# Second attention's results leave PSUM as a high and a low part, and the first weights of the next two products are loaded and split one stage earlier

## The reference, cut to what matters

```python
outs = []
for s0 in range(0, S, Q_BLOCK):              # causal attention, 8 heads
    s = einsum("bqhd,bkhd->bhqk", q[:, s0:e], k[:, :e]) * scale
    p = softmax(where(mask, s, -inf))
    outs.append(einsum("bhqk,bkhd->bqhd", p, v[:, :e]))
o = concatenate(outs).reshape(B, S, 8 * 128)
branch_b = o @ w_mla_o                        # 1024 x 1024
merged = sigmoid(g_a) * branch_a + sigmoid(g_b) * branch_b
h = h + merged @ w_out                        # 1024 x 1024
h = h + hier_moe_2(rmsnorm(h, norm2_g), ...)  # router and experts
```

## Time and profile before

| | us |
|---|---|
| median of three runs (lowest, highest) | 3392.04 (3391.34, 3392.91) |
| the profiled execution's own time | 3380.64 |
| span of its instructions | 3379.1 |
| second attention (`mla_attention`) | from 2294.9 to 2558.8 |
| `merged_product` | from 2559.3 to 2659.7 |
| `residual_norm` of the second block | from 2660.3 on |

### The profile page before, as it was taken

The page is one execution under the profiler, slowest core; times in us unless marked ns, Lnnn a source line. Parts: engine busy times, 40 slices in busy tenths (PEclk is TensorE's granted clock), DMA queues, the critical chain, the costliest instruction groups (busy, mean ns, idle before and its releaser), DMA issues. The chain is left out here.

```text
span 3379.1 us, 41934 instructions
## 1 busy us (share of the span) xinstructions
PE 2882.8 (85%) x16732; PEld 1827.3 (54%) x16732; DVE 1291.4 (38%) x2499; ACT 868.7 (26%) x1446; POOL 309.8 (9%) x490
## 2 busy tenths in 40 slices
PE   5999989777969999994899989787898896878783
PEld 2888667656833333334777877344567772333231
DVE  5321078765731111116365212456554453111113
ACT  5211055573100000005355202233334210100001
POOL 0210000001001110102000000130001101111112
PEclk8999999988979999997999999998999997989897
DMA  7222198042379999976311312200003529999997
GB/s 275 55 81 81 44 412 327 12 164 97 118 287 383 405 405 392 405 322 248 93 46 42 100 60 87 75 11 1 1 1 131 182 97 386 420 420 421 418 414 302
DMA packets 201762, 694.42 MB, mean 206 GB/s; under 512 B 28883, under 2 KB 76934, under 8 KB 151670
## 3 DMA queue, kind: packets, MB, share of 16 engines
q1 hardware_dynamic: 161542, 587.46, 44.8%
q0 software_dynamic: 27520, 75.53, 5.8%
q10 hardware_dynamic: 12528, 29.01, 2.2%
HBM read 579.02 MB, written 138.07 MB: 212 GB/s over the span
## 5 line engine op out<-in xcount | busy, mean ns | idle before, releaser
L2421 PE MATMUL exp_ps_g<-exp_raw,exp_xT 128*32 128x512 f32 x3072 | 337.0, 596 | 9.5 <-ACT exp_xT L2467 9.5
L2725 PE MATMUL exp_ps_g<-exp_gu,exp_xT 128*64 128x512 f32 x992 | 255.1, 673 | 88.3 <-DMA exp_gu<-in_exp_w 83.1
L2421 PEld LDWEIGHTS exp_ps_g<-exp_raw,exp_xT 128*32 128x32 f32 x3072 | 116.8, 110 | 213.7 <-issue 199.3
L2725 PEld LDWEIGHTS exp_ps_g<-exp_gu,exp_xT 128*64 128x64 f32 x992 | 84.3, 154 | 239.3 <-issue 206.7
L724 PE MATMUL inproj_ps<-inproj_w_low,h1T_high 128*128 128x512 f32 (+1 forms) x448 | 178.8, 399 | 9.7 <-DVE inproj_w_low L434 9.7
L726 PE MATMUL inproj_ps<-inproj_w_high,h1T_high 128*128 128x512 f32 (+1 forms) x448 | 175.5, 392 | 0.0
L725 PE MATMUL inproj_ps<-inproj_w_high,h1T_low 128*128 128x512 f32 (+1 forms) x448 | 174.7, 390 | 0.0
L2445 PE MATMUL exp_ps_y<-exp_raw,exp_hT 128*32 128x512 f32 x1536 | 169.8, 592 | 0.8 <-DVE exp_hT L2511 0.8
L2504 DVE TENSOR_TENSOR exp_h<-exp_sg,exp_ps_g 128x512 f32<-128x512 f32 x24 | 26.0, 1085 | 341.9 <-ACT exp_sg L2473 341.9
L2893 DVE TENSOR_TENSOR exp_h<-exp_sg,exp_ps_g 128x256 f32<-128x256 f32 x32 | 19.6, 611 | 337.2 <-ACT exp_sg L2818 337.2
L2757 PE MATMUL exp_ps_y<-exp_dn,exp_hT 128*64 128x512 f32 x512 | 115.8, 592 | 1.5 <-DVE exp_hT L2900 1.5
(11 more groups left out here) (543 smaller groups left out, 5812.1 us busy)
## 6 DMA issues: line engine op xcount, KB each, us to landing
exp_gu<-in_exp_w SPq DMA_DIRECT2D x62, 2048.0 KB, 29.2
exp_raw<-in_expert_w_gate SPq DMA_DIRECT2D x64, 1024.0 KB, 16.6
exp_raw<-in_expert_w_up SPq DMA_DIRECT2D x64, 1024.0 KB, 16.7
exp_raw<-in_expert_w_down SPq DMA_DIRECT2D x64, 1024.0 KB, 15.0
exp_dn<-in_exp_w SPq DMA_DIRECT2D x32, 2048.0 KB, 27.1
scratch_y<-da_zero SPq DMA_DIRECT2D x1, 32768.0 KB, 149.5
scratch_y<-da_zero SPq DMA_DIRECT2D x1, 24576.0 KB, 67.8
open_slab<-in_w_ada SPq DMA_DIRECT2D x16, 1024.0 KB, 14.6
```

Source lines behind the costliest of these rows:

```text
L2421: last = nc.tensor.matmul(ps_g[lane, z], xT[:, n % 2, k, lane], raw[:, of_lane[l], j * F:(j + 1) * F], start=(k == 0), stop=(k == KD - 1))
L2725: last = nc.tensor.matmul(ps_g[side(e)], xT[:, m.par, k, side(e)], gu[:, m.buf, :, e, k, :], start=(k == 0), stop=(k == KD - 1))
```

## The change

The attention's result is no longer copied out of PSUM as it is: ACT casts four heads into the high part of `mla_oT` (`keep_high`), and DVE then makes the low part from PSUM (`keep_low`). Both stand at the end of their iteration, behind the exponentials and the maxima, and `keep_low` waits for `keep_high`. The splitting at the head of `merged_product` is gone. The first slab of `w_mla_o` is loaded and split at the head of `mla_attention` (`FirstSlab`): SP issues it first, ACT splits before its first exponential and DVE before its first maximum. In `merged_product`, SP issues the first three row blocks of `w_out` behind the `ga` of slab 1, and two more at its end; ACT and DVE split two of them behind slabs 2 and 3 (`SplitWeights`). `residual_norm` goes on from there. It takes its weights as four pairs of two blocks each; in the first block's use nothing is loaded or split earlier. The pair `mla_oT` is now placed over `qnT`'s memory.

```diff
-def residual_norm(core, name, hT, w, x, gate, out, gain, shift, rows_out, router, choice, rt, w_pair=None, late=()):
+class SplitWeights:
+    RB, EACH = 3, 2
...
+    def load(self, sp, k):
+        if k >= self.RB:
+            sp.wait_ge(self.split, k - self.RB + 1)
+        sp.dma_start(self.raw[:, k % self.RB], self.rows[:, k]).then_inc(self.loaded[k % self.RB], 16)
+
+    def split_high(self, act, k):
+        act.wait_ge(self.loaded[k % self.RB], 16 * (k // self.RB + 1))
+        self.core.nc.scalar.copy(self.high[k // self.EACH][:, k % self.EACH], self.raw[:, k % self.RB]).then_inc(self.high_done, 1)
+
+    def split_low(self, dve, k):
+        dve.wait_ge(self.high_done, k + 1)
+        high, low = (t[k // self.EACH][:, k % self.EACH] for t in (self.high, self.low))
+        low_part(self.core.nc, low, self.raw[:, k % self.RB], high).then_inc(self.split, 1)
+
+def residual_norm(core, name, hT, weights, x, gate, out, gain, shift, rows_out, router, choice, rt, late=()):
...
-                for k in range(KD):
...
+                for k in range(weights.asked, KD):
+                    weights.load(sp, k)
...
+                for k in range(weights.ready, KD):
+                    weights.split_high(act, k)
...
+                for k in range(weights.ready, KD):
+                    weights.split_low(dve, k)
...
+def mla_attention(core, name, qnT, knT, qrT, krT, v, rq, o_pair, next_slab):
...
+            @block.sync
+            def _(sp):
+                next_slab.load(sp)
...
-                for n in range(0, len(units) + LAG, 2):
-                    if n >= LAG:
+                def keep_high(n):
+                    qt, h = units[n]
+                    if h % 4 == 3:
+                        act.wait_ge(o_done, n + 1)
+                        nc.scalar.copy(high[:, h - 3:h + 1, qt * P:(qt + 1) * P], ps_o[:, h - 3:h + 1]).then_inc(o_high, 1)
+
+                next_slab.split_high(act)
+                for n in range(0, len(units) + LAG + 2, 2):
+                    if LAG <= n < len(units) + LAG:
                         for m in range(2):
                             copy_turned(act, nc.scalar.copy, 0, n - LAG + m)
                     if n < len(units):
                         for m in range(2):
                             exponential(n + m)
+                    if n > LAG:
+                        keep_high(n - LAG - 1)
...
-                def read_results(n):
+                next_slab.split_low(dve)
+                def keep_low(n):
                     qt, h = units[n]
                     if h % 4 == 3:
-                        dve.wait_ge(o_done, n + 1)
-                        V.tensor_copy(qnT[:, h - 3:h + 1, qt * P:(qt + 1) * P], ps_o[:, h - 3:h + 1]).then_inc(o_read, 1)
+                        toks = slice(qt * P, (qt + 1) * P)
+                        dve.wait_ge(o_high, 2 * qt + h // 4 + 1)
+                        low_part(nc, low[:, h - 3:h + 1, toks], ps_o[:, h - 3:h + 1], high[:, h - 3:h + 1, toks]).then_inc(o_read, 1)
...
-                    if n > LAG:
-                        read_results(n - LAG - 1)
...
+                    if n > LAG:
+                        keep_low(n - LAG - 1)
...
+class FirstSlab:
...
+        self.raw = ctx.enter_context(core.nc.sbuf_tensor(f"{name}_raw", [P, KD, P], F32, side="right"))
+        self.high, self.low = pair(core, ctx, f"{name}_w_first", [P, KD, P], "right")
+
+    def load(self, sp):
+        sp.dma_start(self.raw[:], self.w[:, :, 0:P]).then_inc(self.loaded, 16)
+
+    def split_high(self, act):
+        act.wait_ge(self.loaded, 16)
+        self.core.nc.scalar.copy(self.high[:], self.raw[:]).then_inc(self.high_done, 1)
+
+    def split_low(self, dve):
+        dve.wait_ge(self.high_done, 1)
+        low_part(self.core.nc, self.low[:], self.raw[:], self.high[:]).then_inc(self.split, 1)
...
+def merged_product(core, name, oT, first_slab, aT, gT, mT, next_weights):
...
                     if c >= 1:
                         sp.wait_ge(w_split, c)
-                    sp.dma_start(raw[:], wv[:, :, c * P:(c + 1) * P]).then_inc(w_in, 16)
+                        sp.dma_start(raw[:], wv[:, :, c * P:(c + 1) * P]).then_inc(w_in, 16)
...
+                    if c == 1:
+                        for k in range(next_weights.RB):
+                            next_weights.load(sp, k)
+                for k in range(next_weights.RB, next_weights.RB + 2):
+                    next_weights.load(sp, k)
...
                 pe.wait_ge(w_split, 1)
                 for k in range(KD):
-                    pe.wait_ge(o_split, k + 1)
...
-                for k in range(KD):
-                    nc.scalar.copy(o_h[:, k], o[:, k]).then_inc(o_high, 1)
-                    if k == 0:
-                        split(0)
                 split(1)
                 gates(0)
...
                     if c + 2 < KD:
                         split(c + 2)
+                    if c in (2, 3):
+                        next_weights.split_high(act, c - 2)
...
-                for k in range(KD):
-                    dve.wait_ge(o_high, k + 1)
-                    low_part(nc, o_l[:, k], o[:, k], o_h[:, k]).then_inc(o_split, 1)
-                    if k == 0:
-                        split(0)
...
+                    if c in (2, 3):
+                        next_weights.split_low(dve, c - 2)
                 dve.wait_ge(merged, KD)
+        next_weights.asked, next_weights.ready = next_weights.RB + 2, 2
```

More of the change, by code:

```diff
@@ L1775, in number, with __init__, place_raw, place @@
         return nc.gpsimd.memset(self.gp[:], -3.0e38)
-def residual_norm(core, name, hT, w, x, gate, out, gain, shift, rows_out, router, choice, rt, w_pair=None, late=()):
+class SplitWeights:
+    RB, EACH = 3, 2
+    def __init__(self, core, name, w):
+        self.core, self.name = core, name
+        self.rows = w.rearrange("(k p) n -> p k n", p=P)
+        self.loaded = [core.sem(f"{name}_w_in{b}") for b in range(self.RB)]
+        self.high_done, self.split = core.sem(f"{name}_w_high"), core.sem(f"{name}_w_split")
+        self.raw, self.high, self.low = None, [], []
+        self.asked = self.ready = 0
+    def place_raw(self, ctx, side="left"):
+        self.raw = ctx.enter_context(self.core.nc.sbuf_tensor(f"{self.name}_raw", [P, self.RB, D], F32, side=side))
+    def place(self, ctx, upto, side="left"):
+        for k in range(len(self.high) * self.EACH, upto, self.EACH):
+            high, low = pair(self.core, ctx, f"{self.name}_w{k}", [P, self.EACH, D], side)
+            self.high.append(high)
+            self.low.append(low)
+    def load(self, sp, k):
[10 more added lines that the diff above has]
+def residual_norm(core, name, hT, weights, x, gate, out, gain, shift, rows_out, router, choice, rt, late=()):
     nc = core.nc
@@ L1782, in residual_norm @@
     G, GE = wg.shape[1], wg.shape[1] + we.shape[1]
-    wv = w.rearrange("(k p) n -> p k n", p=P)
-    RB, XB, HB = 3, 3, 2
-    w_in = [core.sem(f"{name}_w_in{b}") for b in range(RB)]
+    XB, HB = 3, 2
     x_in = [core.sem(f"{name}_x_in{b}") for b in range(XB)]
@@ L1789, in residual_norm @@
     late_in = core.sem(f"{name}_late_in")
-    w_high, w_split = core.sem(f"{name}_w_high"), core.sem(f"{name}_w_split")
+    w_split = weights.split
     done = core.sem(f"{name}_done")
@@ L1804, in residual_norm @@
         sb = lambda n, s, d=F32: ctx.enter_context(nc.sbuf_tensor(f"{name}_{n}", s, d))
-        raw = sb("raw", [P, RB, D])
-        w_h, w_l = pair(core, ctx, f"{name}_w", [P, KD, D]) if w_pair is None else w_pair
+        if weights.raw is None:
+            weights.place_raw(ctx)
+        weights.place(ctx, KD)
+        raw, w_h, w_l = weights.raw, Joined(weights.high, weights.EACH), Joined(weights.low, weights.EACH)
         xt, yt, ht = sb("x", [P, XB, D]), sb("y", [P, XB, D]), sb("h", [P, HB, D])
@@ L4011, in mla_attention @@
     copied = [sem("copied_act"), sem("copied_dve")]
-    o_done, o_read = sem("o_done"), sem("o_read")
+    o_done, o_high, o_read = sem("o_done"), sem("o_high"), sem("o_read")
+    high, low = o_pair
     barred = sem("barred")
@@ L4181, in merged_product @@
         sb = lambda n, s, d=F32: ctx.enter_context(nc.sbuf_tensor(f"{name}_{n}", s, d))
-        raw = sb("raw", [P, KD, P])
-        w_h, w_l = pair(core, ctx, f"{name}_w", [P, BUF, KD, P])
+        second = pair(core, ctx, f"{name}_w_second", [P, KD, P])
+        w_h, w_l = (first_slab.high, second[0]), (first_slab.low, second[1])
         a, ga, gb = sb("a", [P, BUF, T]), sb("ga", [P, T]), sb("gb", [P, BUF, T])
@@ L4233, in split @@
                         act.wait_ge(done, c - BUF + 1)
-                    nc.scalar.copy(w_h[:, c % BUF], raw[:]).then_inc(w_high, 1)
+                    nc.scalar.copy(w_h[c % BUF][:], raw[:]).then_inc(w_high, 1)
                 def gates(c):
@@ L4269, in split @@
                     dve.wait_ge(w_high, c + 1)
-                    low_part(nc, w_l[:, c % BUF], raw[:], w_h[:, c % BUF]).then_inc(w_split, 1)
```

(20 more changed lines are left out.)

28 lines of the change are left out of this document (10 added, 18 removed).

## The result

The changed kernel took 3397.78 us (median of 14 runs, 3393.67 to 3400.7) against 3391.94 for the one before (14 runs, 3383.7 to 3395.16). The ratio is 1.0024, 95% interval 1.0017 to 1.0031: slower by 5.8 us by the medians and by 8.1 by the ratio, where 3.1 were forecast. That lies in the range. But the forecast called it no difference, with its line at 0.2% or 6.8 us; the measured loss lies about on that line, and an interval that begins at 1.0017 makes it a small loss and not nothing. The profiled execution took 3400.70 us, span 3399.0, 20 us more than the one of before; 10.7 us of these had gathered before the attention stage began (2305.66 in place of 2294.92), ahead of the stages that this text is about. The nine traces that share the change's code there reach that stage between 2297.5 and 2311.6.

The account below looks back on a forecast made before the run. PE was taken to set the pace in the product, with about 36 us of waits in attention; 4.7 + 6.7 - 2.0 - 6.3 = +3.1 on 3392.04 gave 3395.1 us, range 3387 to 3403.

Parts of the forecast that it names:

- Step 1: Head of attention: the first maximum waits behind the first slab's transfer, cast and low part, +4.7 us.
- Step 2: Inside attention: 14 ACT casts at 0.48 us each, between second exponential and copy, delay PE in full, +6.7 us.
- The casts hidden: Rival in attention: PE has other work there, the casts cost 0, sum -3.6 us, 3388.4; chance 0.12.
- DVE's low part: Rival in attention: PE waits for DVE's copy after each `keep_low`, up to +9.5 us, 3404.6; chance 0.10.
- Step 3: First gap and merged product: PE starts 5.4 us earlier, then waits 4 for slab 2's weights; -2.0 us in all.
- the loss of clock behind the stall: Merged product: the clock may fall in the stall at slab 2, losing 2 us once more; half a chance.
- the side chain: Merged product: slower than PE by 0.5 us a slab and 2.4 ahead, bounding the part's gain at -2.9 us.
- The rival of shared transfers: Merged product: transfers share engines, so slab 1's `ga` lands late; part becomes +3.3 us, sum +8.4, 3400.4; chance 0.12.
- Step 4: Second gap, before the residual stage: two row blocks ready, PE starts 5.9 us earlier, clock -0.4; -6.3 us.
- Step 5: `residual_norm` of the first block and the pair over `qnT`: same instructions, only addresses move; no cost.

Follow-up runs that it names:

- e2_slab_late: Changed kernel with the first weight slab still loaded at attention's head but split by ACT and DVE behind its exponentials and maxima: 3389.62 us, 1.0002 to the kernel before.
- e1_cast_early: Changed kernel with ACT's cast of four heads moved ahead of the two exponentials of its iteration: 3388.97 us, ratio 0.9998 to the kernel before.
- the repeated run: The changed kernel measured once more with no edit: 3397.49 us, ratio 1.0027 to the kernel before.
- e3_order: Changed kernel with the three `w_out` row blocks issued behind the third slab's weights instead of ahead of them: 3397.1 us, ratio 1.0024 to the kernel before.
- e5_no_ahead: Changed kernel without any `w_out` row block loaded or split during the merged product: 3402.66 us, ratio 1.0039 to the kernel before.

## Why the prediction was right or wrong

**Step 1, +4.7: right, and short of its consequence.** Measured 4.67, through the very chain that was named. What it lacked is what PE's wait does to the clock: 3.1 us more in B, as `e2_slab_late` shows.

**Step 2, +6.7: right.** A cast costs 0.48 to 0.50 a piece between the second exponential and the copy, and next to nothing ahead of the exponentials (`e1_cast_early`). The casts hidden was the wrong rival. So was DVE's low part: no wait of PE for DVE's copy shows up in the waits of the stage, and the loop's excess is that of the casts.

**Step 3, -2.0: the size.** The gap shrank by 5.45 (5.4 forecast), and the clock stayed up behind it. That was worth 2.2, not 2.0: by the 0.59 of the earlier trace rows the clock before had risen at 2569.8, 4.4 us after PE's restart and not 4.0. From PE's start, `ga` was issued after 14.0 us (14.4), slab 2's weights were ready after 26.6 (26.05), PE came for them at 22.1 (21.8) and waited 4.51 (4). Gap and product together were 96.8 before, 97.3 in the changed kernel's profile and 94.9 in the repeated run, so the part is +0.5 or -1.9: the loss of clock behind the stall, put at half a chance of 2 us, came both times, with 3 and some 1.7. I had also seen that the side chain is slower than PE by 0.5 a slab and taken it as a bound of the gain. It was more than that: with the stall gone it took the same time back (`e3_order`, `e5_no_ahead`). The rival of shared transfers didn't come: `ga` was in use 3.18 us after its issue, with four transfers behind it (2599.99 to 2603.17).

**Step 4, -6.3: right.** The gap shrank by 5.86; behind it the residual stage took 0.1 to 2.2 less, where 0.4 was forecast for the clock. That spread is the clock: F had 12.3 to 12.4 us at the lower level in the three traces with 121.5 or 121.6, 16.8 and 17.0 in the two with 122.6 and 122.8, and 17.5 to 17.9 in the five with 123.3 to 123.7, that of before among them. With this part out, `e5_no_ahead` lost 4 to 5.

**Step 5, nothing: no cost shows.** The first block's use of `residual_norm` took 126.3 us before, from its first product to the router's first, 128.2 in the changed kernel, and 126.1 and 126.3 in `e2_slab_late` and `e3_order`, which have the same code there.

**The sum.** Forecast +3.1; the parts A to F give +7.7 and +7.1. The missing 4 are the clock inside attention, for which the sum had no term at all: B is 10.4 longer, 6.7 to 6.9 of it casts. In the repeated run the other parts came as forecast to 0.3; in the changed kernel's own trace the product's part was 2.5 above its forecast and step 4's 1.7 below. That the total still lay in the range is owed to its width of 16 us, drawn for other rivals. The step that failed is the sentence of step 1 that ends at 4.7, which prices a wait of PE at its own length, whereas in step 3 I had asked of each stall what the clock does behind it. It is a matter of size; the places and signs were right. That PE's wait at the head brings it is shown by the column "low": 34.1 to 37.5 us in the six traces with that wait and the late casts, 20.5 in the three without the wait, with late casts or early ones. Why the early casts take part of it back where the wait remains (27.3) is open.

## What to carry to other kernels

Work moved to an earlier stage goes into an engine's list at a place, and the place is the price: 14 casts cost 6.7 us in front of a copy that PE waits for, and next to nothing behind it. Whatever waits for a transfer doesn't belong at the head of a stage where everything hangs on the same engine, even if it is to be ready early: issue it at the head, use it at the tail. When a removed stall brings no gain, add up the ring that the next waits belong to, from one issue to the next of the same buffer, and compare it with the time of the bounding engine; two delays may hide each other, and only both edits together show it.

## What the runs showed of the hardware

- The 4.7 us that the head of attention grew by, all of it a wait of PE, kept the clock at the lower level for 14 to 17 us longer (34.1 and 37.5 in place of 20.5), and that cost two thirds of the added wait once more (3.1 us in B). In the dense product PE was back at the full clock 6.1 us after its restart (3.7 in the repeated run).
- A cast from PSUM to `fp32r` cost ACT what a plain copy of the same 128 x 512 does: 0.57 to 0.59 alone, 0.46 to 0.48 between two starts in a row.
- DVE made little headway beside POOL in the product where both its inputs lie in SBUF. Its addition of 128 x 1024 took 2.93 us in the changed kernel where POOL's multiplication lay beside it for 1.84 us, and 1.22 where it didn't; the low part in the ring took 1.72 with POOL beside its first 0.64 us, 1.23 without, and that half microsecond counts in the ring. Its product with `mout_ps`, one input from PSUM, lost nothing: 1.23 with POOL beside it all the time, the first row here:

```profile
2598.38 1.23 DVE L4346 TENSOR_TENSOR mout_gb<-mout_ps,mout_gb 128x1024 f32<-128x1024 f32 x1 [2.10 <-ACT mout_gb L4311]
...
2627.41 2.41 POOL L4331 TENSOR_TENSOR mout_a<-mout_a,mout_ga 128x1024 f32<-128x1024 f32 x1 [9.40 <-ACT mout_ga L4309]
...
2627.98 2.93 DVE L4349 TENSOR_TENSOR mout_a<-mout_a,mout_gb 128x1024 f32<-128x1024 f32 x1
...
2638.97 1.22 DVE L4349 TENSOR_TENSOR mout_a<-mout_a,mout_gb 128x1024 f32<-128x1024 f32 x1
```

The Trainium skill (GPSIMD Engine Reference, section "1. Specifications") says that the two engines share SBUF interfaces and that DVE's instructions with two SBUF inputs contend with POOL; these rows agree.
